# Seven half-size products in place of eight in three sections of the last token block of a gated encoder layer, with another order of the first loads and small jobs

## The reference

```
proj = rmsnorm(x) @ w_in                      # 1024 -> 12*512 + 4*1024
out_a = gmlp_spatial(a_u, layernorm(a_v)) * silu(a_z)
out_b = silu(layernorm(dwconv31(b_a * sigmoid(b_b)))) * silu(b_z)
out_c = pool(c_x) * silu(c_z)
out_d = d_b * dwconv3(d_c * d_x) * silu(d_z)
merged = sum over the branches of sigmoid(gate_logits + b_gate) * (out @ w_branch)
x = x + rmsnorm(merged @ w_out)
```

## Time and profile before

| | us |
|---|---|
| median of 3 runs (2459.72 to 2461.53) | 2460.78 |
| the profiled execution | 2460.2 |
| its span, first to last instruction | 2458.1 |
| TensorE matmul busy | 2434.8 |
| VectorE busy | 1258.1 |
| ScalarE busy | 393.5 |
| GpSimd busy | 329.2 |

### The profile page before, as it was taken

How to read it: one execution, slowest core, us unless ns; L and a number is a source line. 1 busy time by engine, 2 the same in 40 slices (tenths; PEclk the granted TensorE clock), 3 DMA queues, 4 the chain that set the end, 5 groups by cost and what they waited for, 6 DMA issues and landing times.

```text
span 2458.1 us, 34054 instructions
## 1 busy us (share of the span) xinstructions
PE 2434.8 (99%) x12772; PEld 2116.8 (86%) x12772; DVE 1258.1 (51%) x1923; ACT 393.5 (16%) x602; POOL 329.2 (13%) x173
## 2 busy tenths in 40 slices
PE   9999999999999999999999999999999999999998
PEld 7888887788888888888888888888899999999997
DVE  6776878752535455643344455654144545554323
ACT  5222222323011000111101000010201100000101
POOL 5435444444000000001000000000200000000000
PEclk9999999999999999999999999999999999999999
DMA  8868887787644555555654555555554344444457
GB/s 320 313 240 298 299 297 283 256 291 268 242 177 171 205 202 207 207 180 205 250 194 163 200 198 217 185 197 197 211 199 156 131 168 177 149 165 171 151 181 280
DMA packets 120382, 528.57 MB, mean 215 GB/s; under 512 B 11664, under 2 KB 14096, under 8 KB 74192
## 3 DMA queue, kind: packets, MB, share of 16 engines
q1 hardware_dynamic: 106032, 502.21, 57.1%
q10 hardware_dynamic: 14240, 24.89, 2.8%
HBM read 409.02 MB, written 118.03 MB: 214 GB/s over the span
## 4 chain that ended last, share of the span: by engine, by line
PE 96%; DVE 2%; issue 1%; DVEq 0%; POOL 0%; DMA 0%; ACT 0%; POOLq 0%; ACTq 0%
PE acc L1231 82%; PE acc L1474 6%; PE side L1369 4%; PE acc L1334 1%; PE side L1396 1%; PE side L1386 1%; PE side L1256 0%; DVE cb L791 0%; PE acc L1375 0%; PE side L1277 0%; DVE tmp L1026 0%; POOL w_pair L402 0%; DMA col<-in_cols 0%; DVE sq_y L1124 0%; DVE merged L1029 0%
## 5 line engine op out<-in xcount | busy, mean ns | idle before, releaser
L1231 PE MATMUL acc<-h_hi,w_pair 128*128 128x512 f32 (+1 forms) x5984 | 1553.3, 353 | 0.0
L1231 PEld LDWEIGHTS acc<-h_hi,w_pair 128*128 128x128 f32 x5984 | 1027.0, 188 | 142.3 <-issue 3.6
L1231 PE MATMUL acc<-h_lo,w_pair 128*128 128x512 f32 (+1 forms) x2992 | 951.4, 351 | 0.0
L1231 PEld LDWEIGHTS acc<-h_lo,w_pair 128*128 128x128 f32 x2992 | 529.3, 188 | 72.2 <-issue 3.6
L791 DVE SCALAR_TENSOR_TENSOR cb<-glu,col,cb 128x512 f32<-128x512 f32 x600 | 396.1, 725 | 23.2 <-issue 18.6
L1231 PE MATMUL acc<-out_hi,w_pair 128*128 128x512 f32 (+1 forms) x1280 | 346.5, 352 | 5.0 <-DVE tmp L1026 5.0
L402 POOL TENSOR_TENSOR w_pair<-w_raw,w_pair 128x512 fp32r<-128x512 f32 (+1 forms) x119 | 272.2, 2299 | 278.5 <-ACT w_pair L500 264.8
L1231 PEld LDWEIGHTS acc<-out_hi,w_pair 128*128 128x128 f32 x1280 | 221.3, 188 | 36.1 <-DVE tmp L1026 6.3
L1026 DVE TENSOR_TENSOR tmp<-acc,sig 128x512 f32<-128x512 f32 (+1 forms) x96 | 68.0, 708 | 342.2 <-PE acc L1231 340.3
L416 POOL TENSOR_TENSOR rstd<-msq,nhalf 128x5 f32<-128x5 f32 (+3 forms) x18 | 19.1, 1063 | 1648.0 <-DVE msq L725 797.7
L510 ACT ACTIVATE sig<-acc,col 128x512 f32<-128x512 f32 (+1 forms) x128 | 90.0, 703 | 896.3 <-PE acc L1231 894.3
(11 more groups left out here) (173 smaller groups left out, 1458.9 us busy)
## 6 DMA issues: line engine op xcount, KB each, us to landing
w_pair<-split_main SPq DMA_DIRECT2D x272, 1024.0 KB, 4.8
split_main<-w_pair SPq DMA_DIRECT2D x88, 1024.0 KB, 6.5
w_pair<-split_branch SPq DMA_DIRECT2D x96, 512.0 KB, 3.7
w_raw<-in_w_main SPq DMA_DIRECT2D x88, 512.0 KB, 5.1
split_branch<-w_pair SPq DMA_DIRECT2D x32, 512.0 KB, 6.5
w_raw<-in_w_branch SPq DMA_DIRECT2D x32, 256.0 KB, 5.6
xr<-in_x_t ACTq DMA_DIRECT2D x3, 2048.0 KB, 13.2
out_y_t<-xr ACTq DMA_DIRECT2D x6, 1024.0 KB, 7.7
```

Source lines behind the costliest of these rows:

```text
L1231: ins = pe.matmul(acc[:, s, b, 0:m], wt[slot][:, wk], mv_[:, k, t0:t0 + m], start=(k == 0 and n == 0), stop=(k == nk - 1 and n == 2))
```

## The change

**Products.** In the last block, D, G1 and G3 are worked in pairs of full tiles: 8, 4 and 4 pairs. A pair of tiles (256 outputs x 1024 inputs) times h (1024 x 576) is cut into 2 x 2 blocks of 128 x 512 by 512 x 288, and the four results come from seven products with four sums of weight blocks (S), four sums of h blocks (T) and seven sums of results on VectorE (`pair_sums`). ScalarE copies the first product out of PSUM (`copy_p1`), as its bank is used again by the fifth. A chunk is one weight block of 512 KB; eight chunk buffers lie over the four tiles of `w_pair`. D uses `acc` and `side` in turn for its pairs, G1 and G3 use `acc`, with `side` for the branch units.

**S.** In blocks 1 and 2, for 8 pairs each, SP loads two raw tiles, GpSimd forms the sums, ScalarE and GpSimd split them, and SP stores 2 MB to `s_parts`. The loads of the layer-norm rows into `w_raw` move to the last block.

**T.** VectorE forms and splits the T blocks during G0 of the last block, ScalarE casts them.

**Taps.** In the last block four of D's taps go ahead of the V statistics, and D has four instead of eight.

**Start.** Tile 0 is loaded ahead of x, SP no longer waits for x, `col` is loaded ahead of `ident`, ScalarE makes tile 0's high part first, VectorE its low part. There are 20 dummies, with a wait for the high part after 12. The two small jobs move from ahead of units 2 and 3 to their middle.

**Loops.** SP's and ScalarE's loops after block 0, and VectorE's merges in the last block, are written out.

```diff
+SEVEN = ["D", "G1", "G3"]
+PAIR0, CHUNK0, PAIR_TILE = {}, {}, []
+_c = 0
+for _n in SEVEN:
+    PAIR0[_n], CHUNK0[_n] = len(PAIR_TILE), _c
+    _k = dict(SECTIONS)[_n] // (4 if _n[0] == "G" else 2)
+    PAIR_TILE += [MAIN0[_n] + 2 * _p for _p in range(_k)]
+    _c += _k * (9 if _n[0] == "G" else 7)
+NPAIR = len(PAIR_TILE)
+NCHUNK = _c
...
+    s_hi = sb("s_hi", [P, 2 * DM], F32R, addr=raw_at)
+    s_lo = sb("s_lo", [P, 2 * DM], F32R, addr=raw_at + 2 * DM * 4)
...
+    chunk = [sb(f"chunk{c}", [P, 2, WB], F32R, addr=pair_at + c * 2 * WB * 4) for c in range(CHUNKS)]
+    s_parts = nc.dram_tensor("s_parts", (NPAIR, P, 2, 4 * WB), F32).ap()
...
+        if name == "D" and p % 2:
+            return [side[:, n // 2, n % 2 * 512:n % 2 * 512 + HALF] for n in range(4)]
+        return [acc[:, n // 2, n % 2, 0:HALF] for n in range(4)]
...
+        n = (it - 4) // 2
+        if 0 < j < NBLK - 1 and it >= 4 and n < NPAIR // 2:
+            return (j - 1) * (NPAIR // 2) + n, (it - 4) % 2
+        return None, None
...
-        for b in range(KT // 2):
-            sp.dma_start(xr[:, 2 * b:2 * b + 2, 0:BLK], x_t[:, 2 * b:2 * b + 2, 0:BLK]).then_inc(x_loaded[b], 16)
-            if b == 0:
-                raw_load(0, 0, raw_rows(MAIN0["B"]), DM)
-        for b in range(KT // 2 - 1):
-            sp.wait_ge(x_loaded[b], 16)
+        raw_load(0, 0, raw_rows(MAIN0["B"]), DM)
...
+        def s_load(q):
+
+            if q == 0:
+                sp.wait_ge(w_lo_done, UPB)
+            else:
+                sp.wait_ge(s_stored, 32 * q)
+            for t in range(2):
+                sp.dma_start(w_raw[t][:, :], raw_rows(PAIR_TILE[q] + t)).then_inc(s_loaded, 16)
+
+        def s_store(q):
+
+            sp.wait_ge(s_lo_done, 2 * q + 2)
+            for n, part in enumerate((s_hi, s_lo)):
+                sp.dma_start(s_parts[q, :, n, :], f(part)).then_inc(s_stored, 16)
...
+            if n - CHUNKS >= (0 if name == "G1" else CHUNK0[name]):
+                sp.wait_ge(chunk_done, n - CHUNKS + 1)
+            else:
+                sp.wait_ge(acc_done, u0 - RING + slot // 2 + 1)
+            sp.dma_start(f(chunk[slot]), src).then_inc(chunk_landed[slot], 16)
...
+            srcs = [a11, s[1], s[2], s[0], a12, s[3], split_main[g + 1, :, :, WB:DM]]
+            if name[0] == "G":
+                m = 2 * (q - PAIR0[name])
+                srcs += [split_branch[GATED[name][0] * KT + m + t, :, :, :] for t in range(2)]
...
+                        if phase == 0 and r == 0:
+                            s_load(q)
+                        if phase == 1 and r == 2:
+                            s_store(q)
...
+                        if j == NBLK - 1 and i == 0 and name in ("G2", "O"):
+                            sp.wait_ge(chunk_done, last_chunk(CHUNK0["G3"] if name == "G2" else NCHUNK, r) + 1)
+                            sp.dma_start(f(w_pair[r])[:, :, 0:n], src).then_inc(w_landed[r], 16)
+                        else:
+                            split_load(u, r, src, n)
...
-        lo(0, 0, DM)
...
+            pool.tensor_tensor(s1, a21, a22, ALU.add)
+            pool.tensor_tensor(s3, a11, a21, ALU.subtract)
+            pool.drain()
+            pool.tensor_tensor(s2, s1, a11, ALU.subtract)
+            pool.drain()
+            pool.tensor_tensor(s4, a12, s2, ALU.subtract)
+            pool.drain().then_inc(s_summed, 1)
+            for t in range(2):
+                pool.wait_ge(s_hi_done, 2 * q + t + 1)
+                pool.tensor_tensor(s_lo[:, t * DM:(t + 1) * DM], w_raw[2 + t][:, :], f(s_hi)[:, t * DM:(t + 1) * DM],
+                                   ALU.subtract).then_inc(s_lo_done, 1)
...
+                    if name == "M" and not last:
+                        for q in range((j - 1) * (NPAIR // 2), j * (NPAIR // 2)):
+                            s_pair_sums(q)
...
+            if p and (name == "D" or p == PAIR0["G1"]):
+                act.wait_ge(pair_used, 2 * p)
+            elif p > PAIR0[name]:
+                act.wait_ge(pair_sig, sigs_before(name, p))
+            act.wait_ge(chunk_done, chunks_before(name, p) + 1)
...
-        for dst, src in [(ident[:, :], ident_in), (col[:, :], cols)]:
+        for dst, src in [(col[:, :], cols), (ident[:, :], ident_in)]:
             act.dma_start(dst, src).then_inc(first_loaded, 16)
 
         act.wait_ge(halo_zeroed, 1)
         act.activation(halo_g[:, 0, :], halo_g[:, 0, :], ACT.Square)
+        hi(0, 0, DM)
         act.wait_ge(first_loaded, 32)
         for k in range(KT):
             act.wait_ge(x_loaded[k // 2], 16)
             act.activation(xg_hi(k), xr[:, k, 0:BLK], ACT.Copy, scale=c1("g_pre", k)).then_inc(xg_hi_done, 1)
-            if k == 1:
-                hi(0, 0, DM)
         hi(1, 1, DM)
         for k in range(KT):
             act.activation(merged[:, k, 0:BLK], xr[:, k, 0:BLK], ACT.Square).then_inc(sq_ready, 1)
...
+        w_low(0)
...
-            for t in range(4):
+            for t in range(8 if last else 4):
...
+                if m == 0:
+                    dve.wait_ge(v_stored, 16)
+                    dve.tensor_tensor(t[1], b12[0], b11[0], ALU.subtract)
+                    dve.drain()
...
+            def pair_sums(name, p):
+
+                n = chunks_before(name, p)
+                bank = banks(name, p)
+                dve.wait_ge(p1_copied, p + 1)
+                dve.wait_ge(chunk_done, n + 2)
+                dve.tensor_tensor(c12, bank[1], c22, ALU.add).then_inc(pair_summed, 1)
+                dve.wait_ge(chunk_done, n + 3)
+                dve.drain()
+                dve.tensor_tensor(c21, bank[2], c12, ALU.add).then_inc(pair_summed, 1)
+                dve.wait_ge(chunk_done, n + 5)
+                dve.tensor_tensor(c11, bank[0], c22, ALU.add)
+                dve.drain()
+                dve.tensor_tensor(c12, bank[3], c12, ALU.add)
+                dve.tensor_tensor(c22, bank[3], c21, ALU.add).then_inc(pair_summed, 2)
+                dve.wait_ge(chunk_done, n + 6)
+                dve.drain()
+                dve.tensor_tensor(c12, bank[1], c12, ALU.add).then_inc(pair_summed, 1)
+                dve.wait_ge(chunk_done, n + 7)
+                dve.tensor_tensor(c21, bank[2], c21, ALU.add).then_inc(pair_summed, 1)
+
...
+            def seven_d(i):
+
+                e = ext[0]
+                p = PAIR0["D"] + 2 * i
+                dve.tensor_copy(e[:, 0:SH], halo_d[:, i, :])
+                dve.tensor_copy(e[:, SH + BLK:2 * SH + BLK], smp_d[:, i, :])
+                pair_sums("D", p)
+                dve.drain()
+                dve.tensor_tensor(e[:, SH:SH + BLK], zc[0][:, 0:BLK], zc[1][:, 0:BLK], ALU.mult)
+                dve.tensor_tensor(e[:, 2 * SH + BLK:2 * SH + BLK + DEC], zc[0][:, BLK:WMAX], zc[1][:, BLK:WMAX], ALU.mult)
+                dve.drain().then_inc(pair_used, 2)
+                for tap in range(3):
+                    for t0, m, c0 in segments(j, SH):
+                        src, dst = e[:, c0 - SH + tap:c0 - SH + tap + m], tmp[:, t0:t0 + m]
+                        if tap == 0:
+                            dve.tensor_scalar(dst, src, c1("short_w", i * 3), None, ALU.mult)
+                        else:
+                            dve.scalar_tensor_tensor(dst, src, c1("short_w", i * 3 + tap), dst, ALU.mult, ALU.add)
+                    dve.drain()
+                dve.tensor_copy(halo_d[:, i, :], e[:, BLK:BLK + SH])
+                dve.tensor_copy(smp_d[:, i, :], e[:, SH + BLK + DEC:2 * SH + BLK + DEC])
+                conv_step(j, 18 + i)
+                pair_sums("D", p + 1)
+                if i == CT - 1:
+                    banks_free()
+                dve.drain()
+                dve.tensor_tensor(tmp[:, :], tmp[:, :], zc[0][:, :], ALU.mult)
+                dve.wait_ge(pair_sig, sigs_before("D", p + 1) + 1)
+                dve.drain()
+                dve.tensor_tensor(tmp[:, :], tmp[:, :], sig[0][:, :], ALU.mult)
+                dve.drain()
+                dve.tensor_tensor(tmp[:, :], tmp[:, :], zc[1][:, :], ALU.mult)
+                dve.drain().then_inc(pair_used, 2)
+                result(j, 0, i)
...
-        for _ in range(14):
+        for n in range(20):
+            if n == 12:
+                pe.wait_ge(w_hi_done, 1)
...
-                if u == 2 and k == 0:
+                if u == 2 and k == KT // 2:
                     square_job(0, SIDE["H", 0], sq_x)
-                if u == 3 and k == 0:
+                if u == 3 and k == KT // 2:
                     row_job(0, SIDE["H", 0] + 1, split=False)
...
+            def product(n, rhs, bank):
+
+                landed(n)
+                wt = chunk[slot_of(n)]
+                for k in range(CT):
+                    for c, (w_part, r_part) in enumerate(((0, 0), (0, 1), (1, 0))):
+                        ins = pe.matmul(bank, wt[:, w_part, k * P:(k + 1) * P], rhs[r_part][:, k, :],
+                                        start=(k == 0 and c == 0), stop=(k == CT - 1 and c == 2))
+                ins.then_inc(chunk_done, 1)
...
```

(61 more changed lines are left out.)

258 lines of the change are left out of this document (223 added, 35 removed).

## The result

The changed kernel takes **2438.26 us** (median of 5 runs, 2436.72 to 2438.77) against 2460.78: a ratio of 0.9907, 95% interval 0.9896 to 0.9919. The forecast was 2438.

The account below looks back on a forecast made before the run. TensorE's matmuls were taken to bound the kernel, busy 2434.8 of 2458.1 us. The terms -25.6 + 3.3 + 2.0 + 1.0 - 3.4 = -22.7 us gave 2438 us against the median of 2460.78, with a range of about 2430 to 2450.

Parts of the forecast that it names:

- Products: Last block's D, G1 and G3: 192 fewer matmuls at 133.4 ns each, -25.6 us, all on the path.
- Sums in D: D: TensorE waits 0.8 us for VectorE's first sum of the odd pair in four rounds, +3.3 us.
- Sums in G1 and G3: Last block's gate sections: VectorE finishes its sums before TensorE needs the banks, cost 0.
- T matrices in G0: Last block's G0: VectorE's eight steps end at D+2.3, needed at D+3.2, cost 0.
- moved taps: Four conv_steps moved ahead of the V statistics start these 1.9 us later, covered by VectorE's idle time, cost 0.
- Chunks: D: a 512 KB chunk takes about 1.34 us of the 1.60 available, cost 0, bound +8.4 us.
- the rival at 299 GB/s: D: chunks come too slowly, +8.4 us, 2446 us in all; chance 0.10.
- Ring at O: Start of O: w_pair[1] loads only at G3's end and lands late, +2.0 us, bounds +1.4 and +5.
- the buffer that is gone isn't won back quickly: O after its first late tile: DMA share already 1.00, so lateness persists; +1.4 us taken as +2.0.
- Stores: Blocks 1 and 2: weight tiles queue behind S stores with under 1 us slack in six places, +1.0 us, bounds 0 and +8.
- GpSimd beside VectorE in blocks 1 and 2: Blocks 1 and 2: GpSimd's new work slows VectorE, but off the path, so 0.
- Start: Block 0's start: earlier first matmul and clock staying at 1.00, less a 1.4 us wait for GpSimd, -3.4 us.

Follow-up runs that it names:

- split_taps: The changed kernel with D's conv_step in halves, two channels between the pairs of a round and two behind it: 2435.20 us in one run.
- extra_chunk: The changed kernel with two more reads of 256 KB in each D pair, into buffers unused there, 8 chunks of traffic for 7: 2438.77 us.
- both mends: The changed kernel with D's conv_step in halves and G3's chunk slots turned by two: 2431.01 us, ratio 0.988 to the kernel before.

## Why the prediction was right, by its own steps

- **Products, -25.6.** The cadence is 132.5 ns (11.13 us for 84) against the 133.4 that were used; with the stall taken off, D and the gate sections give -26.8 instead of -25.6: the matmuls that stay are a little faster too. By the formula of the Trainium skill ("TensorE: Matmul & The Clock Gate", Back-to-back issue gap) an estimate for a pair is 10.3 us, and the trace again does not agree.
- **Sums in D, +3.3.** Measured: four waits, 0.92 us each between matmul starts, +3.6. Mechanism and size held; split_taps removes them.
- **Sums in G1 and G3, T matrices in G0, moved taps, 0 each.** No row of waits names them. G0's piece is 76.98 us for 576 matmuls, and 1758.41 to 1950.30 is 191.89 us beside 191.90 before.
- **Chunks, 0.** No wait. The rate forecast (328 GB/s) is right at 320, and the rival at 299 GB/s is refuted by the 365 of extra_chunk. One figure was wrong: I took 3.7 us from issue to landing, and it is 6.2. The ring of 11.2 us hid it.
- **Ring at O, +2.0.** The first wait is 1.14 us of idle time and 1.4 in matmul starts, as forecast. The second is 1.19 idle and 1.4 in starts, and three unit edges at which the tile lands just in time add 0.5, where I had allowed 0.6 in all for the rest: +3.2 against the kernel before, inside the bounds. The step that was mis-sized is "the buffer that is gone isn't won back quickly". With both mends the small part stays (195 matmuls in 26.66 us, 26.12 before): tiles land at 2380.36, 2383.69 and 2387.04 there, each 0.13 to 0.14 us ahead of its unit.
- **Stores, +1.0.** Measured 0. The slack was 2.0 us in five of six places instead of under 1. The step that was mis-sized is the landing: counted from the start of the group, the stores landed at +3.6 instead of +5.1 and the tile behind them at +6.1 instead of +7.7 (796.41 and 798.93, the group beginning at 792.79).
- **GpSimd beside VectorE in blocks 1 and 2, 0.** The 240 conv operations there mean 928 ns instead of 747, and the stretch is as long as before. It is off the path, as written.
- **Start, -3.4.** Measured -2.8 at unit 6 and -1.2 in block 1. Order, clock and the wait for GpSimd (1.2 us, forecast 1.4) came as written. Tile 3 was ready 0.24 us later than taken and the work behind it ran 0.4 longer, and the piece at 444 was outside the sum altogether.

The sum was -22.7 and the profiled span gave -21.2: misses of -1.2, +0.3, +1.2, -1.0, +0.6 and +1.6 us, of both signs. The median of 2438.26 against a forecast of 2438 is closer than the terms were: they cancel in part.

## What to carry to other kernels

Where one engine is 99% busy, count the instructions taken away times their cadence in the chain, then follow every new consumer and every reused buffer to the moment it is due; here that found both new waits, and mending them gave a quarter as much again as the change itself. An order by hand should be looked at for the last user of a buffer at a section's end: turning the slots by two was one term in one line, and took 2 us. When an experiment adds load, read its own chain before its total, or its own waits pass for a limit of the chip.

## What the runs showed of the hardware that was not expected

- The same pause of TensorE at 442 us (2.02 us idle) is followed by 3.4 us at 1.2 GHz in some executions and by none in others (4.61 or 3.01 us for 12 matmuls). The last six matmuls of the kernel behave alike: 1.77 us at a granted clock of 0.50 in the changed kernel's profile, 1.03 at 1.00 in that of its repeat. 1.6 and 0.74 make up the 2.4 us between the two spans (2436.9 and 2434.5).
- A DMA share of 0.95 in 320 GB/s was not full: 365 GB/s followed with 14% more traffic, and no wait. The landing time grew well before: the median for 512 KB is 3.8 us for the branch tiles and 6.2 for the chunks.
- A single VectorE addition of 0.69 us took 2.73 beside one GpSimd instruction of 2.52. The two overlapped for 2.18 us, and the addition lost 2.04: not a share of that time but nearly all of it. A second such pair is alike (2.75 beside 2.66).
